# Decode attention with four heads in the four 32-column parts of TensorE's array

## What is computed

```
q, k: (stream, token, head 8, map 2, 64)      v: (stream, token, head 8, 128)
k, v = concatenate([cache of 512 rows, 16 new rows])
s = einsum('bqhmd,bkhmd->bmhqk', q, k) * 64 ** -0.5
p = softmax(s, axis=-1)
a = p[:, 0] - lam * p[:, 1]
o = einsum('bhqk,bkhe->bqhe', a, v)
```

## Time and profile before

| | us |
|---|---|
| median of 3 runs | 4133.78 |
| lowest and highest | 4129.03, 4146.48 |
| span of the profiled execution | 4137.5 |
| PE busy in it | 3636.2 (88%) |
| DVE busy | 1786.9 (43%) |
| ACT busy | 1234.8 (30%) |

### The profile page before, as it was taken

The page is one execution under the profiler, slowest core; times in us unless marked ns, Lnnn a source line. Parts: engine busy times, 40 slices in busy tenths (PEclk is TensorE's granted clock), DMA queues, the critical chain, the costliest instruction groups (busy, mean ns, idle before and its releaser), DMA issues. The chain is left out here.

```text
span 4137.5 us, 53520 instructions
## 1 busy us (share of the span) xinstructions
PE 3636.2 (88%) x19236; PEld 3217.7 (78%) x19237; DVE 1786.9 (43%) x2037; ACT 1234.8 (30%) x1321; POOL 695.6 (17%) x428
## 2 busy tenths in 40 slices
PE   5999999999998988887999756999999999999950
PEld 5999999999997656667999754777777777777740
DVE  4111111001112326662111245667888868747655
ACT  4000000000000114541000114556776756646542
POOL 1222232222221001323222111010000100101000
PEclk7999999999999988988999757999999999999975
DMA  3111111122223421112333437877999969958667
GB/s 130 46 52 51 46 52 57 63 70 86 80 63 133 170 99 40 48 42 64 86 86 86 136 136 240 293 261 283 332 327 344 337 240 357 339 202 306 232 256 286
DMA packets 396185, 678.52 MB, mean 164 GB/s; under 512 B 40346, under 2 KB 236186, under 8 KB 383087
## 3 DMA queue, kind: packets, MB, share of 16 engines
q1 hardware_dynamic: 320724, 573.33, 39.8%
q10 hardware_dynamic: 62395, 61.95, 4.6%
q0 software_dynamic: 13024, 42.71, 2.8%
HBM read 629.39 MB, written 92.56 MB: 174 GB/s over the span
## 5 line engine op out<-in xcount | busy, mean ns | idle before, releaser
L1721 DVE TENSOR_TENSOR e_w_lo<-expert_raw,e_w_hi 128x2048 fp32r<-128x2048 f32 x388 | 887.7, 2291 | 342.3 <-ACT e_w_hi L1667 332.3
L1667 ACT ACTIVATE e_w_hi<-expert_raw 128x2048 fp32r<-128x2048 f32 x388 | 743.3, 1916 | 406.1 <-PE e_gu L1598 328.8
L266 PE MATMUL p_z<-hT_hi,p_w_hi 128*128 128x384 f32 x2304 | 772.2, 335 | 10.0 <-POOL p_w_lo L254 10.0
L267 PE MATMUL p_z<-hT_lo,p_w_hi 128*128 128x384 f32 x2304 | 770.8, 335 | 0.0
L268 PE MATMUL p_z<-hT_hi,p_w_lo 128*128 128x384 f32 x2304 | 770.7, 334 | 0.0
L266 PEld LDWEIGHTS p_z<-hT_hi,p_w_hi 128*128 128x128 f32 x2304 | 433.3, 188 | 10.1 <-issue 10.1
L267 PEld LDWEIGHTS p_z<-hT_lo,p_w_hi 128*128 128x128 f32 x2304 | 433.3, 188 | 0.0
L268 PEld LDWEIGHTS p_z<-hT_hi,p_w_lo 128*128 128x128 f32 x2304 | 433.3, 188 | 0.0
L1598 PE MATMUL e_gu<-e_w_hi,e_xT_hi 128*128 128x512 f32 x1216 | 378.2, 392 | 24.2 <-issue 24.2
L699 ACT ACTIVATE d_kT<-d_t 128x512 f32<-128x512 f32 x32 | 19.0, 595 | 1274.2 <-PE d_t L575 1274.2
L1598 PE MATMUL e_gu<-e_w_lo,e_xT_hi 128*128 128x512 f32 x1216 | 375.3, 390 | 0.0
(11 more groups left out here) (251 smaller groups left out, 4640.3 us busy)
## 6 DMA issues: line engine op xcount, KB each, us to landing
expert_raw<-w_ei SPq DMA_DIRECT2D x260, 1024.0 KB, 7.0
expert_raw<-w_eo SPq DMA_DIRECT2D x128, 1024.0 KB, 7.4
p_w_raw<-w_in SPq DMA_DIRECT2D x96, 512.0 KB, 3.9
f_r<-expert_rows SPq DMA_DIRECT2D x18, 1024.0 KB, 10.5
d_k<-cache_k SPq DMA_DIRECT2D x8, 2048.0 KB, 12.5
d_v<-cache_v SPq DMA_DIRECT2D x8, 2048.0 KB, 7.9
m_w_raw<-w_out SPq DMA_DIRECT2D x32, 512.0 KB, 4.1
chunks<-p_e ACTq DMA_DIRECT2D x24, 576.0 KB, 2.8
```

Source lines behind the costliest of these rows:

```text
L266: pe.matmul(out, w_hi[:, k, :], x_hi[:, xk, cols], start=(k == 0), stop=False)
L267: pe.matmul(out, w_hi[:, k, :], x_lo[:, xk, cols], start=False, stop=False)
L1667: act.activation(w_hi[:, s, :], raw[:, r, :], ACT.Copy).then_inc(hi_done, 1)
L1721: dve.tensor_tensor(w_lo[:, s, :], raw[:, r, :], w_hi[:, s, :], ALU.subtract).then_inc(lo_done[r], 1)
```

## The change

`phase_decode` is rewritten; nothing else changes but the place of its call, which now stands ahead of the allocation of the tiles `o_hi` and `o_lo`. 

- Scores: each head has 32 stationary columns (`qx` is [P, STREAMS, HEADS, 32], written once for all streams by two DVE copies) and writes 32 partitions of `s_ps` that are its own, W * j for head j of the group. The new keys of all streams are loaded once, to `kn`, and are no longer behind the cached ones in `kT`.
- Values: the loop over the blocks of keys is now outside that over the heads. Head j has 32 stationary columns (16 are zero) and writes partitions W * j of `o_ps`. The block of new rows has 128 rows, of which 112 are zero, cleared once by POOL.
- The loop over streams is written out on every engine. SP issues the first keys ahead of the queries; the waits for stream b - 2 stay.
- The result goes out in four DMAs a stream, issued by POOL, from two buffers `orow`.

```diff
+        qx = sb("d_qx", [P, STREAMS, HEADS, W])
+        at = sb("d_at", [P, PT + 1, HG, W])
+        orow = sb("d_orow", [P, 2, G, VD])
 @block.sync
+                load_keys(0)
                 sp.dma_start(qs[:], io.chunks[CH:2 * CH, :, PROMPT:TOK].rearrange("h p n -> p h n")).then_inc(q_loaded, 16)
+                sp.dma_start(kn[:], io.chunks[2 * CH:3 * CH, :, PROMPT:TOK].rearrange("h p n -> p h n")).then_inc(kn_loaded, 16)
+                load_keys(1)
+                load_values(0)
+                load_values(1)
+                for b in range(2, STREAMS):
+                    load_keys(b)
+                    load_values(b)
 @block.gpsimd
+                for b in range(STREAMS):
+                    pool.wait_ge(o_kept, G * (b + 1))
+                    for j in range(HG):
+                        pool.dma_start(io.o_new[b * NEW:(b + 1) * NEW, :].rearrange("q (g j e) -> j q g e", g=G, j=HG)[j],
+                                       orow[W * j:W * j + NEW, b % 2, :, :]).then_inc(o_stored[b % 2], 16)
 def scores
-                    for lo, hi in ((0, PAST), (PAST, KEYS)):
-                        for j in range(HG):
-                            h = hg * HG + j
-                            mm = pe.matmul(s_ps[:, hg, lo:hi], qx[:, h, :], kT[:, s, h, lo:hi], start=(j == 0), stop=(j == HG - 1))
+                    for j in range(HG):
+                        h = hg * HG + j
+                        pe.matmul(s_ps[W * j:W * (j + 1), hg, 0:PAST], qx[:, b, h, :], kT[:, b % 2, h, :], start=True, stop=True)
+                    for j in range(HG):
+                        h = hg * HG + j
+                        mm = pe.matmul(s_ps[W * j:W * (j + 1), hg, PAST:KEYS], qx[:, b, h, :], kn[:, h, b * NEW:(b + 1) * NEW],
+                                       start=True, stop=True)
 def values
-                    for j in range(HG):
-                        cols = slice((hg * HG + j) * VD, (hg * HG + j + 1) * VD)
-                        for t in range(PT + 1):
-                            w = min(P, KEYS - t * P)
-                            rhs = v[:, s, t, cols] if t < PT else vn[:, s, cols]
-                            mm = pe.matmul(o_ps[0:NEW, j * VD:(j + 1) * VD], at[0:w, t, j * NEW:(j + 1) * NEW], rhs,
-                                           start=(t == 0), stop=(t == PT))
+                    for t in range(PT + 1):
+                        for j in range(HG):
+                            cols = slice((hg * HG + j) * VD, (hg * HG + j + 1) * VD)
+                            rhs = v[:, b % 2, t, cols] if t < PT else vn[:, b % 2, cols]
+                            mm = pe.matmul(o_ps[W * j:W * (j + 1), 0:VD], at[:, t, j, :], rhs, start=(t == 0), stop=(t == PT))
...
```

More of the change, by code:

```diff
@@ L487, in phase_decode @@
     HG = 4
+    G = HEADS // HG
     KEYS = PAST + NEW
     PT = PAST // P
+    W = 2 * NEW
     with ExitStack() as mem:
@@ L518, in by_stream @@
[L518 to L524, removed]
+        scores_done, bias_ready, exp_done = sem("d_scores_done"), sem("d_bias_ready"), sem("d_exp_done")
+        rl_ready, mixl_ready = sem("d_rl_ready"), sem("d_mixl_ready")
+        at_done, at_kept, o_done, o_kept = sem("d_at_done"), sem("d_at_kept"), sem("d_o_done"), sem("d_o_kept")
@@ L526, in phase_decode @@
+        last = STREAMS - 1
         with nc.Block() as block:
@@ L539, in load_values @@
[L539 to L555, removed]
@@ L562, in _, with turn_keys @@
+                for s in range(2):
+                    pool.wait_ge(o_stored[s], 16 * HG * (STREAMS // 2))
             @block.tensor
             def _(pe):
[L564 to L568 removed]
+                def turn_keys(b, heads):
                     for h in heads:
                         if h == 0:
[L571 to L573 removed]
+                            pe.wait_ge(k_loaded[b % 2], 16 * (b // 2 + 1))
+                        if b * HEADS + h >= 2:
+                            pe.wait_ge(kT_ready[h % 2], b * (HEADS // 2) + h // 2)
@@ L607, in values @@
                     mm.then_inc(o_done, 1)
[L609 to L612, removed]
+                turn_keys(0, range(HEADS))
+                pe.wait_ge(qx_ready, 2)
+                pe.wait_ge(kn_loaded, 16)
+                for b in range(STREAMS):
                     for part in range(2):
[L614 to L619, removed]
+                        pe.wait_ge(kT_ready[part], (b + 1) * (HEADS // 2))
+                    scores(b, 0)
+                    scores(b, 1)
+                    if b < last:
+                        turn_keys(b + 1, range(0, 4))
@@ L620, in stream @@
                     mix(b, 0)
-                    if more:
-                        turn_keys(*nx, range(4, 6))
-                    values(b, i, s, 0)
+                    if b < last:
+                        turn_keys(b + 1, range(4, 6))
+                    values(b, 0)
                     mix(b, 1)
[L625 to L630, removed]
+                    if b < last:
+                        turn_keys(b + 1, range(6, 8))
@@ L632, in _, with keep_keys, bias @@
+                    values(b, 1)
             @block.vector
             def _(dve):
+                def keep_keys(b, heads):
+                    for h in heads:
+                        dve.wait_ge(k_turned, b * HEADS + h + 1)
+                        dve.tensor_copy(kT[:, b % 2, h, :], t_ps[:, 1, :]).then_inc(kT_ready[1], 1)
+                def bias(b, hg):
+                    dve.wait_ge(scores_done, b * G + hg + 1)
+                    dve.tensor_reduce(nb[:, hg:hg + 1], s_ps[:, hg, 0:KEYS], AX.X, ALU.max, negate=True).then_inc(bias_ready, 1)
@@ L640, in _ @@
                 dve.wait_ge(mixer_step, 2)
-                dve.wait_ge(qx_zeroed, 1)
+                dve.wait_ge(zeroed, 3)
                 dve.wait_ge(q_loaded, 16)
[L643 to L658, removed]
-                    dve.tensor_reduce(nb[:, hg:hg + 1], s_ps[:, hg, 0:KEYS], AX.X, ALU.max, negate=True).then_inc(bias_ready, 1)
-                def over_sum(b, hg):
-                    n = b * G + hg
-                    dve.wait_ge(exp_done, n + 2)
-                    dve.reciprocal(rl[:, hg:hg + 1], l[:, hg:hg + 1]).then_inc(step, 1)
-                    dve.wait_ge(step, n + 1)
-                    dve.tensor_scalar(mixl[:, hg, :], mixer[:], rl[:, hg:hg + 1], None, ALU.mult).then_inc(mixl_ready, 1)
-                def keep_mixed(b, hg):
-                    dve.wait_ge(at_done, b * G + hg + 2)
-                    w = PT * HG * NEW
-                    dve.tensor_copy(at[:, 0:PT, :].rearrange("p a b -> p (a b)"), at_ps[:, 0:w])
-                    dve.tensor_copy(at[0:NEW, PT, :], at_ps[0:NEW, w:w + HG * NEW]).then_inc(at_kept, 1)
-                def stream(i, s, more):
-                    b, nx = 2 * i + s, 1 - s
+                for m in range(2):
+                    part = slice(m * DH, (m + 1) * DH)
+                    dve.tensor_copy(qx[part, :, :, m * NEW:(m + 1) * NEW],
+                                    qs[part, :, :].rearrange("p h (b q) -> p b h q", b=STREAMS)).then_inc(qx_ready, 1)
+                keep_keys(0, range(1, HEADS, 2))
+                for b in range(STREAMS):
                     bias(b, 0)
@@ L707, in keep_rows @@
                 def keep_rows(b, hg):
-                    act.wait_ge(o_done, b * G + hg + 2)
-                    if hg == 0:
-                        act.wait_ge(o_stored, 16 * b + 1)
-                    act.activation(orow[:, hg * 512:(hg + 1) * 512], o_ps[0:NEW, :], ACT.Copy).then_inc(o_kept, 1)
-                def stream(i, s, more):
-                    b, nx = 2 * i + s, 1 - s
+                    act.wait_ge(o_done, b * G + hg + 1)
+                    if hg == 0 and b >= 2:
+                        act.wait_ge(o_stored[b % 2], 16 * HG * (b // 2))
+                    act.activation(orow[:, b % 2, hg, :], o_ps[:, 0:VD], ACT.Copy).then_inc(o_kept, 1)
+                keep_keys(0, range(0, HEADS, 2))
+                for b in range(STREAMS):
                     exps(b, 0)
                     exps(b, 1)
-                    if more:
-                        keep_keys(b + 1, nx, (0, 2, 4))
+                    if b < last:
+                        keep_keys(b + 1, (0, 2, 4))
                     keep_rows(b, 0)
-                    if more:
-                        keep_keys(b + 1, nx, (6,))
+                    if b < last:
+                        keep_keys(b + 1, (6,))
                     keep_rows(b, 1)
-                    act.wait_ge(o_kept, G * (b + 1) + 1)
-                    act.dma_start(io.o_new[ds(b * NEW, NEW), :], orow[:]).then_inc(o_stored, 16)
-                keep_keys(0, 0, range(0, HEADS, 2))
-                by_stream(act, stream)
 def phase_attend(c, a_hi, a_lo, o_hi, o_lo):
```

109 lines of the change are left out of this document (62 added, 47 removed).

## The result

| | before | after |
|---|---|---|
| median, us | 4138.72 (4 runs) | 4013.21 (4 runs) |
| lowest, highest | 4129.03, 4146.48 | 4002.89, 4022.61 |
| profiled span | 4137.5 | 4016.1 |
| first scores of the phase | 1318.39 | 1317.03 |
| next phase's first instruction | 1540.40 | 1423.04 |

The ratio is 0.970 (95% interval 0.9675 to 0.9724). Forecast were 4083 us with a range of 4036 to 4126: the sign is right and the size wrong, the gain being 125.5 us for the 50.6 forecast. Of the 121.4 us between the spans 116.0 lie in the phase and 1.4 ahead of it. The other 4 are in phases that nothing changed; those differ by 16 us between two profiles of the changed kernel (this one and v11). The phase itself repeats well: 106.0 us in both.

What follows compares the result with a forecast made beforehand. PE, the matrix engine, was taken to bound the decode phase. Seven streams 132.3, the last 16.5, end 6.6 and clock 16 made 171.4 us against 222.0, a saving of 50.6: 4083 us, range 4036 to 4126.

Steps and rivals of the forecast that it cites:

- part 1: Scores in the decode phase: only neighbouring records of different heads overlap, 2.5 us a group, 5.0 a stream (before 8.56).
- The term for the scores, 5.0: Scores of both head groups in one stream: 5.0 us, for 8.56 before.
- the two terms of 3.0: Values of the first and second head group in a stream: 3.0 us each, for 5.18 before.
- Rival 1: Four column parts run side by side: stream 12.9 us, phase 123, saving 99, kernel 4035 us; chance 13%.
- The clock: PE's clock in the decode phase: a fall costs 3.2 us, expected in five of eight streams, 16 us.
- (b): Section of a stream turning the next stream's heads 0 to 5, first mixing product between: kept at 5.48 us.
- Loads: Key and value loads of the decode streams: 10.3 us a stream, keys wanted 24 us after issue, so hidden.
- (d): Section of a stream with the second mixing product and two more heads turned: kept at 2.27 us.
- the narrow score products: Score records with 16 moving columns: 0.03 us each with 32 columns to load, 0.24 for eight.
- the start: Start of the decode phase: first scores at 1318.39 again, zero change, plus or minus 1.5 us.
- The end: After PE's last values: ACT's copy 0.6, four POOL issues 3.0, landing 2 to 4, 6.6 us (before 3.0).
- rival 3: Slower: each change of column part drains the array, 0.10 us, 45 us in all, kernel 4163 us; chance 6%.

Runs made afterwards that it cites:

- v11: The changed kernel run again with no edit: 4009.31 us, ratio 0.9705.
- v2: The changed kernel with all heads' scores and values in the first column part, values head by head (outputs wrong): 4102.95 us, ratio 0.9905.
- v1: The changed kernel with only the order of value records changed, a head's ten coming together: 4037.76 us, ratio 0.9756.
- v8: The changed kernel with values ordered by pairs, heads 0 and 1 in turn through all blocks, then 2 and 3: 4017.37 us, timed once.
- v5: The changed kernel with the next stream's keys loaded ahead of the current stream's values, from stream 1 on: 4005.46 us, ratio 0.9682.
- v10: The changed kernel with values ordered as two blocks of each head, two more of each, then the new rows: 4013.07 us, timed once.
- v6: The changed kernel loading only the first quarter of the values from stream 2 on (outputs wrong from there): 4020.67 us, timed once.
- v9: The changed kernel with new rows as 16 rows, not padded to 128: 4007.51 us, timed once.
- v12: The changed kernel with values ordered as three blocks of each head, then the two left of each: 4012.03 us, timed once.
- v3: The changed kernel with the old scores put back, 128 stationary columns and sums over four heads: 4068.30 us, ratio 0.983.
- v4: The changed kernel with the old values put back and their single store, issued by POOL: 4071.14 us, ratio 0.984.

## Why the prediction was wrong

**The step that failed is in part 1:** "the two of one instruction use the same part and are neighbours in a queue that starts multiplies in order. Only the second record of a head and the first of the next can overlap, so four heads need 5 slots, not 8." It was taken from the order of the records in a trace in which no two neighbours could have run at once (the scores used all the columns, the values always the same ones), and so could not tell whether a waiting record holds the ones behind it. It does not, as long as its part has room: the scores took 2 slots, not 5, and a value group 10, not 21. The term for the scores, 5.0, measured 1.94, and the two terms of 3.0 measured 1.23 and 1.12. Over seven streams that is 7 x (3.1 + 1.8 + 1.9) = 48 us, and 7 more in the last. v2 shows that the parts make this difference, and v1 and v8 how far a record may pass. The forecast's 171.4 us were 132.3 + 16.5 + 6.6 + 16; the 106.0 measured are 7 x 11.9 = 83.3, then 9.7, 7.0, and 6.0 of waits for keys and clock. v1 shows what is right in it: starts do hold back in the wrong order (3.27 us a group for 1.23), though less than strictly (4.17).

**Rival 1**, with 13%, was the case that came: 12.9 a stream (measured 11.9), the last 10.5 (9.7), end 6.6 (7.0). Without its 16 us of clock its sum is 107; the phase took 106.0, though that agreement is partly luck, since 6.0 of it are waits for keys and clock that the sum did not have. The forecast's range ended at 4036 us, one above this rival's own 4035. Its argument against, the order of the records, should have made no more than an even bet, since no row showed two parts at work.

**The clock** was the second miss: one fall for five. The share of (b) in a stream had been taken as what makes the clock fall. (b) is 45% of the stream now, and in v5 the granted clock is 1.00 in every stretch of the phase's streams. In all four profiles with a wait for keys of 3.1 to 4.2 us (after, v11, v10, v6) the clock fell behind it, and not behind the waits of up to 2.2 us in v8, v9 and v12. That is not the only way: both falls before, and those in the last streams of v3, v4, v6 and v8, came with no wait over 1.3 us, and v5 had the same waits in its last stream and none. What decides is open. The price of 3.2 us holds for the falls before, each 6.8 us long; it goes with the length (1.6 us for 3.4, 4.35 for 9.4), so one price for every fall was wrong, and the two falls inside the 222.0 are 6.3 us, not about 8.

**Loads** did not stay hidden: 7.0 us of waits, 4.1 in one. The working had 24 us between issue and need, from a stream of 18.9; the stream came out at 12, while 4.2 MB at about 400 GB/s take 10.5, and keys 2, issued at 1316.2 and wanted at 1331, stood behind two value loads. v5 gives the time back.

**Right:** (b) 5.33 for 5.48, (d) 2.28 for 2.27, where PE waits for ACT's copy as before; the narrow score products at 0.03; the start, -1.4 in a range of 1.5, though other profiles of the same start differ by as much. The end, 7.0 for 6.6, is two misses that cancel (POOL's issues 0.50 each for 0.74, landing 4.4 for 2 to 4). **Not borne out:** rival 3's drain for each change of part. The twenty changes of a value group at 0.10 would be 2.0 us, and the whole group takes 1.23.

**The pages.** The Trainium skill (TensorE: Matmul & The Clock Gate, Measured speedup vs the span model) has 2.38 times for three parts; here four gave 3.68 / 0.92 = 4.0 for the scores and 4.4 / 1.23 = 3.6 for the values, and no run has three. The prediction had noted that this figure points near rival 1, and gave that rival 13% all the same. The same page of the Trainium skill (The mechanism) has multiplies start strictly in program order, which agrees with the step that failed; v1's row with ten value records contradicts both. By the same section of the Trainium skill, weight loads overlap running multiplies only where the row group differs. Here 32 loads of 0.110 us, all with the same 128 rows, fit into the 0.81 us from 1352.70, beside each other and beside the group's multiplies.

## What to carry to other kernels

Where products have at most 32 stationary columns and separate outputs, give each of four its own 32 columns and let the instructions go round the four parts; the order counts (1.23 us a group round the heads, 3.27 head by head), but two products of a head in a row (four records) cost next to nothing (v10, 1.27). An order seen in a trace in which all the work used one resource says nothing on what several will do, so its two ends deserve even chances. When a stage comes down to less than half, work out again whether its loads still fit: 4.2 MB take 10.5 us, of 26.7 us a stream before and of 11.9 now. When they only just fit, issue first what is wanted first (v5).

## What the hardware showed that was not expected

- A record in one column part passes up to three waiting records of another (v1: 3.27 us a group, for 4.17 by strict order; v8: 1.90).
- Four 512-column fp32 products in four parts start within 0.02 us and run at once, each reading its own moving data: a group of scores takes 0.92 us, and 3.68 in one part (v2).
- Products with 16 moving columns take 0.03 us a record in 32 stationary columns and 0.10 in 128 (v2: 1345.37 to 1345.62 for eight; v3: 0.81 us for eight).
- The granted clock fell to 0.50 after an idle of 4.1 us for keys, for 3.4 us, and after one of 3.1 us (v6) for 10. With 1.1 us idle a stream it stayed at 1.00 in v5, but in v6 it fell once more in the last stream, after idles of 1.24 and 0.64 us.
